# A gate buffer of 1040 elements in place of 1028, which shifts all SBUF tiles behind it by 32 bytes

## What is computed

```python
u = rms_norm(h, g_mix)
z = u @ w_in                                   # 1024 -> 512 (lru) + 512 (gate) + 512 (pool)
y_lru = rg_lru(causal_dwconv(z_lru), ...) * gelu(z_gate)
y_pool = multiscale_pool(z_pool, ...)
h = h + concat(y_lru, y_pool) @ w_out
v = rms_norm(h, g_ffn)
up = causal_dwconv(v @ w_up, w_conv_ffn)       # 1024 -> 2 * 3072
h = h + (gelu(gate) * val) @ w_down
q = rms_norm(h, g_ple)
h = h + sigmoid(q @ w_ple_gate + b_ple_gate) * (p @ w_ple_proj)
return rms_norm(h, g_final)
```

## Time and profile before

| | |
|---|---|
| median of 3 runs | 2322.22 us |
| the profiled execution's own time | 2321.61 us |
| its span, first to last instruction | 2319.8 us |
| mean granted TensorE clock | 0.983 |
| TensorE matmul busy | 2227.3 us (96%), 9416 matmuls |
| TensorE weight load busy | 1775.3 us (77%), 9416 loads |
| VectorE busy | 1550.3 us (67%) |
| ScalarE busy | 1021.4 us (44%) |
| DMA | 154.81 MB, mean 67 GB/s |

### The profile page before, as it was taken

One profiled execution on the slowest core, in us unless ns is written; L12 is line 12 of the kernel. 1 busy time (PEld: TensorE's weight loads), 2 busy tenths in 40 slices (PEclk: granted clock), 3 DMA queues, 4 the chain that ended last, 5 costly groups with the idle time before them and its releaser, 6 DMA issues.

```text
span 2319.8 us, 24242 instructions
## 1 busy us (share of the span) xinstructions
PE 2227.3 (96%) x9416; PEld 1775.3 (77%) x9416; DVE 1550.3 (67%) x1754; ACT 1021.4 (44%) x1397; POOL 0.2 (0%) x4
## 2 busy tenths in 40 slices
PE   7999989999999999999889999899999999999995
PEld 5777768888888888887667787688888888888873
DVE  6774397575848485776767735966757575848755
ACT  5763355352525252554545624534435342525532
POOL 0000000000000000000000000000000000000000
PEclk9999999999999999999999999999999999999997
DMA  3114211121211111133121143021211121211221
GB/s 138 41 46 145 77 65 58 38 72 37 69 41 57 34 55 55 55 127 109 55 100 46 37 154 114 30 66 37 69 41 55 39 71 37 69 41 55 75 84 73
DMA packets 72002, 154.81 MB, mean 67 GB/s; under 512 B 7760, under 2 KB 7888, under 8 KB 71888
## 3 DMA queue, kind: packets, MB, share of 16 engines
q1 hardware_dynamic: 69584, 144.87, 18.9%
q10 hardware_dynamic: 2304, 8.39, 0.9%
HBM read 136.45 MB, written 16.78 MB: 66 GB/s over the span
## 4 chain that ended last, share of the span: by engine, by line
PE 85%; DVE 8%; ACT 4%; issue 2%; DMA 1%; SPq 0%; ACTq 0%; DVEq 0%
PE slot L427 47%; PE slot L500 37%; DMA raw<-panels 1%; DVE wlo L972 1%; DVE H L1062 1%; DVE UN L1160 1%; DVE ops L1165 1%; DVE UN L1172 1%; ACT whi L598 0%; PE slot L456 0%; ACT L606 0%; ACT ops L743 0%; DVE H L1124 0%; DVE ops L1177 0%; DVE XQ L997 0%
## 5 line engine op out<-in xcount | busy, mean ns | idle before, releaser
L500 PE MATMUL slot<-ops,whi 128*128 128x512 f32 x2576 | 813.3, 397 | 18.8 <-ACT WG L792 12.8
L500 PEld LDWEIGHTS slot<-ops,whi 128*128 128x128 f32 x2576 | 484.3, 188 | 140.3 <-ACT WG L792 13.7
L500 PE MATMUL slot<-ops,wlo 128*128 128x512 f32 x1288 | 510.1, 396 | 0.0
L598 ACT ACTIVATE whi<-raw 128x512 fp32r<-128x512 f32 x370 | 228.2, 625 | 508.0 <-PE slot L427 325.8
L427 PE MATMUL slot<-f_split,whi 128*128 128x512 f32 x1536 | 420.6, 395 | 0.0
L427 PEld LDWEIGHTS slot<-f_split,whi 128*128 128x128 f32 x1536 | 287.9, 187 | 70.5
L972 DVE TENSOR_TENSOR wlo<-raw,whi 128x512 fp32r<-128x512 f32 x370 | 249.0, 687 | 76.6 <-ACT whi L598 75.3
L500 PEld LDWEIGHTS slot<-ops,wlo 128*128 128x128 f32 x1288 | 242.5, 188 | 59.5
L598 ACT ACTIVATE whi<-wsum 128x512 fp32r<-128x512 f32 x184 | 115.4, 627 | 329.7 <-DVE wsum L968 186.7
L1314 DVE TENSOR_TENSOR H<-slot,H 128x1024 f32<-128x1024 f32 x96 | 117.3, 1222 | 196.7 <-PE slot L427 196.7
L427 PE MATMUL slot<-f_split,wlo 128*128 128x512 f32 x768 | 241.4, 395 | 0.0
(11 more groups left out here) (156 smaller groups left out, 2222.9 us busy)
## 6 DMA issues: line engine op xcount, KB each, us to landing
raw<-panels SPq DMA_DIRECT2D x416, 256.0 KB, 2.7
XN<-xT SPq DMA_DIRECT2D x8, 1024.0 KB, 9.2
H<-xT SPq DMA_DIRECT2D x8, 1024.0 KB, 9.7
pp_kept<-XQ ACTq DMA_DIRECT2D x16, 512.0 KB, 2.7
PPR<-pp_kept SPq DMA_DIRECT2D x16, 512.0 KB, 3.8
outT<-H SPq DMA_DIRECT2D x16, 512.0 KB, 3.0
WG<-pT SPq DMA_DIRECT2D x2, 512.0 KB, 12.6
WV<-pT SPq DMA_DIRECT2D x2, 512.0 KB, 14.3
```

The source lines that it names most:

```text
L500: mm = pe.matmul(ps, stat_[:, w], (lo if part else hi)[:, k, :], start=first and k == 0 and i == 0, stop=k == KP - 1 and i == 2, skip_grou ...
L598: nc.scalar.activation(whi[n % RING][:], source(n), ACT.Copy).then_inc(panel_hi, 1)
```

## The change

The base of the layout is rounded up to 64 bytes in place of 32, and WG is declared 1040 elements wide in place of 1028. 1028 x 4 = 4112 bytes are placed as 4128; 1040 x 4 = 4160 bytes are placed as 4160. No other line is touched, and the slices of WG that are read and written stay the same.

```diff
-        base = (nc.sbuf_base + 31) // 32 * 32
+        base = (nc.sbuf_base + 63) // 64 * 64
...
-        WG = place("WG", [P, BLOCK + 4])
+        WG = place("WG", [P, BLOCK + 16])
```

## The result

The changed kernel takes 2269.79 us (median of 4 runs, 2269.2 to 2270.76) against 2322.11 us of the kernel before on the same chips (2321.0 to 2322.71): a ratio of 0.9776, 95% interval 0.9759 to 0.9793. The forecast was no change; the range of 2308 to 2332 does not hold it.

What follows compares the result with a forecast made beforehand. The prediction took TensorE's matmuls times their pitch as the bound. Its terms summed to 0, with 0.2 us either way for VectorE and ScalarE and 0.2 for DMA, so 2322.2 us, unchanged; range 2308 to 2332 us.

Steps and rivals of the forecast that it cites:

- The bound: TensorE's split products: 9,384 matmuls at a pitch of 233.3 ns, 2,189 us, 94% of the span; 1 ns is 9.4 us.
- VectorE, ScalarE, DMA, the moving operand in the statistics: Other users of shifted tiles: 0 each, with 0.2 us either way for VectorE and ScalarE and 0.2 us for DMA.
- The first edited line moves nothing: Base of the layout: first free byte 1121 rounds up to 1152 by 32 and by 64 alike, so no address changes.
- TensorE's weight loads: 0, bounds -20 and +3.3 ns: All 9,384 loads of whi or wlo: no change taken from the nearest row; a gain could reach 188 us.
- rival 1: Weight loads: at 32 past a multiple, nine 64-byte pieces, not eight; 6.7 ns each, 63 us faster, 2259 us; chance 0.08.
- The model of the pitch: TensorE's split products: 188 ns of weight load plus 45 ns of hand-over, with the moving stream's 213.3 ns as lower limit.
- Rival 2: Weight and moving streams now start in step and share banks: 3.3 ns a load, 31 us slower, 2353 us; chance 0.05.
- The tell named last: Line 500: mean weight load and time per 336 matmuls, 181 ns and 76.2 us if faster, 191 and 79.5 if slower.
- The mean load: Weight loads of line 500: 187 to 188 ns if nothing changes, 181 if faster, 191 if slower.

Runs made afterwards that it cites:

- e1: Kernel before, WG still 1028 wide, 32 bytes skipped ahead of the first whi, so only whi, wlo and small tiles behind move; 2270.35 us, ratio 0.9782.
- e2: Kernel before with WG 1040 wide and 32 bytes skipped ahead of whi: WV to wsum on multiples of 64, split weights 32 past; 2322.27 us, ratio 1.0003.
- m4: Block left out, matmuls alone: 512 to 128 columns at distances 0 and 224, then mixes of distances; 120 and 116.7 ns a matmul at 256 columns.
- e3: Kernel before with the base 32 bytes later: weights on multiples of 64, moving tiles of the products 32 bytes past one; 2322.39 us, ratio 1.0003.
- e4: Kernel before with the base 32 bytes later and WG 1040 wide: weights and moving tiles both 32 bytes past multiples of 64; 2270.76 us, ratio 0.9779.
- n1: Kernel before with 96 bytes skipped ahead of whi: all split weights on multiples of 64, at distance 64 from moving tiles; 2322.47 us, ratio 1.0001.
- m1: Block left out, 3,648 matmuls alone on 38 weight tiles at distances 0 to 496 by 16 and six between; 226.7 ns at 0, 16 and 240.
- m3: Block left out, matmuls alone at eight distances, six batches each in changing order; 226.7 ns in all six at 0, 233.3 in all six at 224.
- e5: Kernel before with 32 bytes skipped ahead of whi and 32 more ahead of wlo: whi at distance 0, wlo at 32; 2315.63 us, ratio 0.9973.

## Why the prediction was wrong

**The bound** was read rightly: matmuls times pitch, 94% of the span, 1 ns of pitch worth 0.4%. That part made the answer legible in one row.

**VectorE, ScalarE, DMA, the moving operand in the statistics:** 0 forecast, 0 found (687, 625, 1.88 us; e1 and e2 leave nothing for the rest). The first edited line moves nothing, as worked out: e1, with that line as it was, has all of the gain.

**The step that failed** is "TensorE's weight loads: 0, bounds -20 and +3.3 ns". The term measured -6.67 ns per matmul. It was taken as 0 since the nearest row, XQ against AV in the statistics, showed no effect. That row could not show one. By 256, the weights `means` lay at 224 from XQ and at 64 from AV, two distances that are slow in float32r; and after the change they lie at 0 from XQ, and the four records still take 1.88 us. So plain float32, at half the column rate (429 ns a matmul), hides the surcharge at every distance it had; the prediction said that it could under rival 1 and did not draw the consequence. The trace of before held no row of the stream in question at another distance, and so the honest reading was an open term of up to 188 us, not a zero with a chance of 0.78. The section on the term kept both bounds for the range; the range of 2308 to 2332 then left them out.

**The model of the pitch** (188 ns of weight load and 45 ns of hand-over) was wrong as well. m4 shows the pitch fall with the columns, to 120 ns at 256, which no chain of 233 ns could do; and after the change the pitch fell while the load's record grew by a ns. The pitch is the moving stream plus a hold-up, with 512 columns of 32 cycles at distance 0 and of 48 in the mean at 224. That the weights' address moves it says that 16 of the cycles have to do with reading them; for the other 32 no run without a load per matmul was made. In the trace of before a load begins with a matmul and the next matmul 0.23 us on the earlier trace rows; that order fits both readings, and I took it for cause. The Trainium skill's TensorE: Matmul & The Clock Gate (Back-to-back issue gap) has N / 2.4 + 2.5 ns for an isolated gap, and says that in a stream of loads and matmuls both set the spacing, which the prediction passed over. Here the slope agrees and the constant is 13.3 ns at best with a load per matmul.

**Rival 1** gave 2259 us from 6.7 ns a load, and 6.67 ns and 2270 us came; but its mechanism (nine pieces of 64 bytes in place of eight, by the weights' own address) is refuted by e3, e4 and n1. The number was right by luck: the mean happened to fall by 16 cycles, the rival's one piece, from another cause. Of the 11 us between its 2259 and the result, 8.6 went to waits and to matmuls at granted clock 0.50, which the rival left out.

**Rival 2** had the right object, the two streams in or out of step, and the wrong sign: in step is what is fast. It also counted the step by 64 and not by 256, so that its rebuttal (statistics with both cases, both 1.88 us) set one slow distance against another, at half rate.

**The tell named last** did its work: 76.2 us per 336 was given for rival 1, and 76.16 came. The mean load, named as the one number that would show it (181 or 191 ns), did not move down at all.

## What to carry to other kernels

Where every matmul has a weight load of its own in float32r and streams of 384 or 512 columns, put the weight tiles at a distance of a multiple of 256 bytes from the tiles that stream past them; here that is worth 6.67 ns, 3% of a matmul of 512 columns, and 32 bytes of padding decide it. With 256 columns distance 0 was the slower of the two tried (120.0 against 116.7 ns in m4). Alignment by 64 for its own sake does nothing. Read the result from starts, over a long piece without waits: the records of the loads did not show it. If a steady pitch is above columns over clock, and no row shows the operands placed otherwise, price the gap as open and not by a slower kind of matmul.

## What the runs showed of the hardware

- In float32r with a weight load for each matmul, the pitch at full clock is columns / 2.4 GHz + 13.3 ns with weights and moving tile at distance 0 by 256 bytes (173.5, 120 ns at 384, 256 columns), and + 20, 16.7 and 10 ns at distance 224 with 512, 384 and 256 columns; with 128 columns both distances are at 111.5 ns (m4).
- In plain float32 the pitch is 429 ns with 512 columns, at distances 0, 64 and 224 alike (the statistics, before and after).
- The distance counts by 256 bytes (each step of 16 from 0 to 240 and again from 256 to 496 in m1); the address by 64 does not (e3, e4, n1). No distance in steps of 4 bytes went below 226.7 ns, so the changed kernel is at the least that placing alone gives in these scans. No kernel run here beat it.
- Some distances have more than one pace: in m3, 16 bytes gave 226.7 ns four times and 233.3 twice, 100 bytes 226.7, 230.0 and 233.3, and a whole kernel at 16 ran in 2297 to 2319 us.
- The record of a weight load (187 to 189 ns in the products' steady groups, at either pitch) does not show the hold-up; only starts do.
- One load of twelve at distance 224 lengthens the step into its matmul to 235 ns and the next to 232 (m4); one of three at distance 32 slows line 500's products to 233.2 in the mean (e5).
- Left open: what in the reads makes the hold-up and why it goes by 256 bytes, why a few distances like 100 and 156 are sometimes good, and whether the 13.3 ns left can be had back with fewer loads, since each matmul of this kernel issues one; that was not tried.
